# Three of four MLP up projections as seven half-size products in place of eight

## The reference

```python
hdn = rmsnorm(x, p["norm_mlp"][i]) @ p["w_up"][i]                 # 1024 -> 4096
x = x + (jnp.square(jax.nn.relu(hdn)) @ p["w_down"][i]).astype(x.dtype)   # 4096 -> 1024
```

## Time and profile before

| what | value |
|---|---|
| median of 3 runs | 2495.04 us (2494.24 to 2495.99) |
| the profiled execution, its own time | 2499.5 us |
| its span, first to last instruction | 2497.7 us |
| PE, DVE, ACT, POOL busy, share of the span | 98%, 39%, 42%, 18% |
| mean granted clock of PE | 0.996 of full speed |
| layer 0's MLP, in the chain of waits | 716.95 to 1252.04 us |
| POOL's accumulating DMAs of 256 KB, issue to landing | median 5.5 us, 504 issues |
| SP's raw chunk loads of 512 KB, issue to landing | median 3.9 us, 258 issues |

### The profile page before, as it was taken

One profiled execution on the slowest core, in us unless ns is written; L12 is line 12 of the kernel. 1 busy time (PEld: TensorE's weight loads), 2 busy tenths in 40 slices (PEclk: granted clock), 3 DMA queues, 4 the chain that ended last, 5 costly groups with the idle time before them and its releaser, 6 DMA issues.

```text
span 2497.7 us, 34597 instructions
## 1 busy us (share of the span) xinstructions
PE 2455.3 (98%) x13260; PEld 2061.6 (83%) x13260; DVE 973.5 (39%) x1372; ACT 1057.0 (42%) x1928; POOL 442.8 (18%) x512
## 2 busy tenths in 40 slices
PE   8999999999999999999999999999999999999996
PEld 6888578888888888888888885887878888888885
DVE  7877675104221111212378777630143211111124
ACT  5544536434443333434435435454344433333343
POOL 1111002220112122222111110023201222222210
PEclk9999999999999999999999999999999999999998
DMA  5544327863456666666555442378616566666664
GB/s 158 108 102 107 99 60 163 186 137 64 89 120 130 123 127 125 121 129 122 107 115 115 101 111 93 84 164 184 122 30 122 118 130 124 124 126 122 130 123 118
DMA packets 119789, 295.50 MB, mean 118 GB/s; under 512 B 13574, under 2 KB 13958, under 8 KB 119636
## 3 DMA queue, kind: packets, MB, share of 16 engines
q0 software_dynamic: 73152, 133.20, 31.9%
q1 hardware_dynamic: 46484, 160.20, 23.5%
HBM read 290.20 MB, written 3.15 MB: 117 GB/s over the span
## 4 chain that ended last, share of the span: by engine, by line
PE 94%; DVE 3%; DMA 2%; ACT 1%; issue 0%; SPq 0%; DVEq 0%; ACTq 0%
PE G L816 74%; PE M L1035 2%; PE G L1217 2%; PE M L775 2%; PE M L786 1%; PE M L788 1%; PE M L787 1%; PE G L1048 1%; PE M L1103 1%; DMA wlo<-wstream 1%; PE G L1013 1%; PE M L763 1%; PE M L932 1%; PE M L940 1%; PE M L831 0%
## 5 line engine op out<-in xcount | busy, mean ns | idle before, releaser
L425 ACT ACTIVATE wlo<-raw 128x512 fp32r<-128x512 f32 x508 | 320.6, 631 | 1101.7 <-PE G L816 1012.1
L411 POOL DMA_DIRECT2D wlo<-wstream x504 | 439.1, 871 | 1904.2 <-ACT wlo L425 1849.8
L816 PE MATMUL G<-A_lo,whi 128*128 128x256 f32 x1888 | 641.8, 340 | 0.0
L816 PE MATMUL G<-A_hi,whi 128*128 128x256 f32 x1888 | 605.8, 343 | 14.9 <-DVE A_lo L1326 9.1
L816 PE MATMUL G<-B_lo,whi 128*128 128x256 f32 (+1 forms) x1536 | 520.2, 339 | 0.0
L816 PE MATMUL G<-B_hi,whi 128*128 128x256 f32 (+1 forms) x1536 | 488.5, 340 | 0.0
L816 PE MATMUL G<-A_hi,wlo 128*128 128x256 f32 x1888 | 482.2, 337 | 0.0
L816 PEld LDWEIGHTS G<-A_hi,wlo 128*128 128x128 f32 x1888 | 356.3, 189 | 86.3
L816 PE MATMUL G<-B_hi,wlo 128*128 128x256 f32 (+1 forms) x1536 | 391.3, 336 | 0.0
L816 PEld LDWEIGHTS G<-A_lo,whi 128*128 128x128 f32 x1888 | 357.9, 190 | 38.7
L816 PEld LDWEIGHTS G<-A_hi,whi 128*128 128x128 f32 x1888 | 357.9, 190 | 21.4 <-issue 15.7
(11 more groups left out here) (304 smaller groups left out, 2436.3 us busy)
## 6 DMA issues: line engine op xcount, KB each, us to landing
raw<-wstream SPq DMA_DIRECT2D x258, 512.0 KB, 3.9
wlo<-wstream POOLq DMA_DIRECT2D x504, 256.0 KB, 5.5
ring<-dft SPq DMA_DIRECT2D x12, 512.0 KB, 3.8
mraw<-memT SPq DMA_DIRECT2D x16, 256.0 KB, 3.4
X<-xT SPq DMA_DIRECT2D x8, 384.0 KB, 6.9
win<-dft SPq DMA_DIRECT2D x6, 512.0 KB, 4.8
itab<-dft SPq DMA_DIRECT2D x6, 512.0 KB, 6.3
yT<-outs SPq DMA_DIRECT2D x8, 384.0 KB, 2.6
```

The source lines that it names most:

```text
L411: pool.dma_start(low, wstream[c][:, part], accum_op=ALU.add).then_inc(lo_in[c % 2][h], 16)
L425: act.activation(wlo[:, s, part], raw[:, s, part], ACT.Copy, scale=-1.0).then_inc(neg_done, 1)
L816: last = mm(out, w, p[:, k, a:b], start=(k == 0 and w is w_hi and p is parts[0]), stop=(k == KT - 1 and w is w_lo))
```

## The change

Quarter 0 of the MLP and all down tiles stay as they are. The up tiles of quarters 1, 2 and 3 of each layer go by groups: a group is two output tiles (256 hidden channels, two rows of `raw`), and takes the product of a 2x2 block weight (blocks of 128 outputs by 512 inputs) with a 2x2 block input (512 inputs by 384 tokens). The Strassen scheme (in Winograd's form) makes it of seven block products where eight are needed plainly. Each of the seven is 4 contraction blocks times three matmuls of 384 columns. A quarter is four groups, 28 products.

- **The inputs.** The norm's scale now goes onto the input: during the first four down tiles of quarter 0, DVE's `combine` makes the normalised input (`x_hat`) and four sums of its blocks (they become `T1` to `T4`) and, with ACT, the high and low parts of all seven input operands. They lie where `A_hi`, `A_lo` and the relu and hidden buffers were. They serve all three quarters.
- **The weights.** A product's weights lie in one of four half slots of `whi` and `wlo`, and are prepared when the product four places before has been used. Products 0, 4 and 6 of a group take a block as it is: negated copy on ACT, accumulating DMA on POOL (product 0's low part has a buffer of its own, `w_low`, prepared six products ahead). Products 1, 2, 3 and 5 take sums of blocks: DVE makes the sum in place in `raw`, ACT rounds it, DVE subtracts for the low part.
- **The results.** Products 0, 1, 2, 3 go to four PSUM banks, 4, 5, 6 are added onto banks 0, 2, 3. ACT copies products 0 and 1 out before 4 and 5 may write, DVE adds 2 and 3; then come the four hidden blocks of 128x384, each with a relu and square, a rounding copy on ACT and a subtraction on DVE.
- **The raw loads** come in pairs of rows, alternately in `raw` and a new `raw_b`.
- The loops over layers and quarters on SP, ACT and DVE are written out.

The core of the diff, with the indentation cut:

```diff
-CH = C_MLP + 16 * QUARTERS
+STREAM = C_MLP + 16 * QUARTERS
+FAST = QUARTERS - 1
+CH = STREAM - 8 * FAST
+LOADS = CH // 2 + 2 * FAST
 AHEAD = 2
 T_IN, T_OUT, T_K, T_Q, T_O, T_MLP = 0, 20, 28, 36, 44, 52
-TILES = T_MLP + 64
+TILES = T_MLP + 64 - 8 * FAST
...
+def combo(i):
+    o = oA + 12288 * i if i < 4 else oE + 12288 * (i - 4)
+    return tuple(place(f"mlp_{n}{i}", [P, 4, HALF_T], o + 6144 * j, F32R) for j, n in enumerate(("hi", "lo")))
+B11, B21, B22, T1, T2, T3, T4 = combos = [combo(i) for i in range(7)]
+x_hat = [place(f"x_hat{i}", [P, T], oE + 36864 + 3072 * i) for i in range(2)]
+t_one, t_two, t_three, t_four = acc[:, 0:HALF_T], acc[:, HALF_T:T], sq[:, 0:HALF_T], sq[:, HALF_T:T]
+raw_b = place("raw_b", [P, 2, D], oE + 36864)
+assert oE + 36864 + 8192 <= 229344
+p_one, p_five, v_sum = acc[:, 0:HALF_T], acc[:, HALF_T:T], sq[:, 0:HALF_T]
...
+def quad(p, row, col):
+    return pair_raw(p)[:, row, col * 512:(col + 1) * 512]
+def part_of(j):
+    return j % 4 // 2, slice(j % 2 * 512, j % 2 * 512 + 512)
...
-chunks(L, C_V0, CH - C_V0)
+chunks(L, C_V0, C_MLP + 16 - C_V0)
+for q in range(1, QUARTERS):
+    U, w = (L * FAST + q - 1) * 4, L * STREAM + C_MLP + 16 * q
+    def pair(p, buf, arrived):
+        for row in range(2):
+            if p > 1:
+                sp.wait_ge(u_dlo, 4 * (U + p - 2) + 4)
+                sp.wait_ge(u_hi, 7 * (U + p - 2) + (6, 7)[row])
+            sp.dma_start(buf[:, row, :], wstream[w + 2 * p + row]).then_inc(arrived[row], 16)
+    if q == 1:
+        sp.wait_ge(c_lo, 28 * (L + 1))
+    else:
+        sp.wait_ge(u_dlo, 4 * U)
+        sp.wait_ge(u_hi, 7 * U)
+    pair(1, raw_b, raw_b_in)
+    pair(2, raw, raw_in)
+    pair(3, raw_b, raw_b_in)
+    pair(4, raw, raw_in)
+    for m in range(8):
+        c = L * CH + C_MLP + 8 + 8 * q + m
+        sp.wait_ge(hi_done, c * 2 + 2)
+        sp.dma_start(raw[:, m % 2, :], wstream[w + 8 + m + AHEAD]).then_inc(raw_in[m % 2], 16)
...
+def first_low(p):
+    pool.wait_ge(u_neg1, U + p + 1)
+    pool.dma_start(w_low[:, :], wstream[w + 2 * p][:, 0:512], accum_op=ALU.add).then_inc(u_lo[0], 16)
+def later_low(p, i):
+    s, part = part_of(7 * p + (4, 6)[i])
+    pool.wait_ge(u_neg, 2 * (U + p) + i + 1)
+    pool.dma_start(wlo[:, s, part], wstream[w + 2 * p + i][:, 512:1024],
+                   accum_op=ALU.add).then_inc(u_lo[1 + i], 16)
+first_low(0)
+for p in range(4):
+    later_low(p, 0)
+    if p < 3:
+        first_low(p + 1)
+    later_low(p, 1)
+for m in range(8):
...
+for i, (src, ready) in enumerate(((x_hat[0][:, 0:HALF_T], 1), (x_hat[1][:, 0:HALF_T], 2), (x_hat[1][:, HALF_T:T], 2),
+                                  (t_one, 3), (t_two, 4), (t_three, 5), (t_four, 6))):
+    act.wait_ge(c_src, n + ready)
+    act.activation(combos[i][0][:, g, :], src, ACT.Copy).then_inc(c_hi, 1)
...
+def first_neg(q, p):
+    arrived, k = arrival(q, p)
+    act.wait_ge(arrived[0], 16 * (k + 1))
+    act.activation(w_low[:, :], quad(p, 0, 0), ACT.Copy, scale=-1.0).then_inc(u_neg1, 1)
+def weight_high(q, j):
+    U, (p, n) = (L * FAST + q - 1) * 4, divmod(j, 7)
+    s, part = part_of(j)
+    arrived, k = arrival(q, p)
+    U += p
+    if n == 6:
+        act.wait_ge(arrived[1], 16 * (k + 1))
+    if n in (1, 2, 3, 5):
+        act.wait_ge(u_s, 4 * U + (2, 1, 3, None, 4)[n - 1])
+    src = quad(p, *((0, 0), (1, 0), (0, 0), (0, 0), (0, 1), (0, 0), (1, 1))[n])
+    if n in (4, 6):
+        act.activation(wlo[:, s, part], src, ACT.Copy, scale=-1.0).then_inc(u_neg, 1)
+    act.activation(whi[:, s, part], src, ACT.Copy).then_inc(u_hi, 1)
+def fast_up(q):
+    U0 = (L * FAST + q - 1) * 4
+    for i in range(28):
+        U, n = U0 + i // 7, i % 7
+        bank = (GB, MB)[i // 7 % 2]
+        act.wait_ge(u_mm, 7 * U0 + i + 1)
+        if i < 24:
+            weight_high(q, i + 4)
+        else:
+            s, part = part_of(i)
+            if i % 2 == 0:
+                act.wait_ge(raw_in[s], 16 * (L * LOADS + (C_MLP + 16) // 2 + 6 * (q - 1) + 2 + 1))
+            act.activation(wlo[:, s, part], raw[:, s, part], ACT.Copy, scale=-1.0).then_inc(neg_done, 1)
+            act.activation(whi[:, s, part], raw[:, s, part], ACT.Copy).then_inc(hi_done, 1)
+        if n == 1 and i < 21:
+            first_neg(q, i // 7 + 1)
+        if n == 0:
+            act.wait_ge(u_c, 3 * U + 1)
+            act.activation(p_one, bank[0][:, 0:HALF_T], ACT.Copy).then_inc(u_p1, 1)
+        if n == 1:
+            act.activation(p_five, bank[2][:, 0:HALF_T], ACT.Copy).then_inc(u_p5, 1)
+        if n == 4:
+            act.activation(h_buf[1], bank[0][:, 0:HALF_T], ACT.Relu).then_inc(u_c11, 1)
+            act.wait_ge(u_c11, U + 1)
+            act.activation(h_buf[1], h_buf[1], ACT.Square).then_inc(u_sq, 1)
+            act.wait_ge(u_sq, U + 1)
+        if n >= 3:
+            k, half, buf, ready = ((1, 1, 0, 1), (0, 0, 1, None), (0, 1, 0, 2), (1, 0, 1, 3))[n - 3]
+            if ready is not None:
+                act.wait_ge(u_h, 3 * U + ready)
+            act.activation(B_hi[:, 2 * (i // 7) + k, half * HALF_T:(half + 1) * HALF_T], h_buf[buf],
+                           ACT.Copy).then_inc(u_hh, 1)
...
+    first = (C_MLP + 8) // 2 if q == 0 else (C_MLP + 16) // 2 + 6 * (q - 1) + 2
+    act.wait_ge(raw_in[s], 16 * (L * LOADS + first + (m + 2) // 2 + 1))
+    split(s, c + m)
+else:
+    if m == 6:
+        first_neg(q + 1, 0)
+    for h in range(2):
+        act.wait_ge((half_used, chunk_used)[h], c + m + 1)
+        weight_high(q + 1, 2 * s + h)
...
+def fast_up(q):
+    U0 = (L * FAST + q - 1) * 4
+    for p in range(4):
+        U, bank = U0 + p, (GB, MB)[p % 2]
+        for n, (src, b) in enumerate(((B11, 0), (T1, 2), (T3, 3), (T2, 1), (B21, 0), (B22, 2), (T4, 3))):
+            j = 7 * p + n
+            s, part = part_of(j)
+            if p == 0 and n == 0:
+                pe.wait_ge(psum_free, L * TILES + T_MLP + 16 + 8 * (q - 1) + 2)
+                pe.wait_ge(c_lo, 28 * (L + 1))
+            if p >= 2 and n < 4:
+                pe.wait_ge(*((u_c11, U - 1), (u_c, 3 * U - 3), (u_c, 3 * U - 2), (u_u1, U - 1))[n])
+            if n >= 4:
+                pe.wait_ge((u_p1, u_p5, u_v)[n - 4], U + 1)
+            pe.wait_ge(u_hi, 7 * U0 + j + 1)
+            if n in (0, 4, 6):
+                pe.wait_ge(u_lo[n // 3], 16 * (U + 1))
+            else:
+                pe.wait_ge(u_dlo, 4 * U + (1, 2, 3, None, 4)[n - 1])
+            out = bank[b][:, 0:HALF_T]
+            for k in range(4):
+                w = part.start + k * P
+                w_hi, w_lo = whi[:, s, w:w + P], wlo[:, s, w:w + P]
+                if n == 0:
+                    w_lo = w_low[:, k * P:(k + 1) * P]
+                mm(out, w_hi, src[0][:, k, :], start=(n < 4 and k == 0), stop=False, skip_group_check=n > 3)
+                mm(out, w_hi, src[1][:, k, :], start=False, stop=False, skip_group_check=n > 3)
+                last = mm(out, w_lo, src[0][:, k, :], start=False, stop=(k == 3), skip_group_check=n > 3)
+            last.then_inc(u_mm, 1)
+    pe.wait_ge(u_c11, U0 + 3)
+    pe.wait_ge(u_c, 3 * U0 + 10)
 up(L * CH + C_MLP, L * TILES + T_MLP, True)
-down(L * CH + C_MLP, L * TILES + T_MLP, L * 32)
+down(0)
 for q in range(1, QUARTERS):
...
+def combine(g):
+    n, k = (L * 4 + g) * 6, (L * 4 + g) * 7
+    if k:
+        dve.wait_ge(c_lo, k)
+    for i in range(2):
+        stt(out=x_hat[i][:, :], in0=X[:, g + 4 * i, :], scalar=par_("g_mlp", g + 4 * i), in1=rbc[:, :],
+            op0=ALU.mult, op1=ALU.mult).then_inc(c_src, 1)
+    b11, b12, b21, b22 = (x_hat[i][:, j * HALF_T:(j + 1) * HALF_T] for i in range(2) for j in range(2))
+    dve.wait_ge(c_src, n + 2)
+    tt(t_one, b12, b11, ALU.subtract).then_inc(c_src, 1)
+    dve.wait_ge(c_src, n + 3)
+    tt(t_two, b22, t_one, ALU.subtract).then_inc(c_src, 1)
+    tt(t_three, b22, b12, ALU.subtract).then_inc(c_src, 1)
+    dve.wait_ge(c_src, n + 4)
+    tt(t_four, b21, t_two, ALU.subtract).then_inc(c_src, 1)
+    for i, src in enumerate((b11, b21, b22, t_one, t_two, t_three, t_four)):
+        dve.wait_ge(c_hi, k + i + 1)
+        tt(combos[i][1][:, g, :], src, f(combos[i][0][:, g, :]), ALU.subtract).then_inc(c_lo, 1)
+def weight_low(q, j):
+    U, (p, n) = (L * FAST + q - 1) * 4, divmod(j, 7)
+    s, part = part_of(j)
+    a11, a12, a21, a22 = (quad(p, i, k) for i in range(2) for k in range(2))
+    if n == 1:
+        arrived, k = (raw_in, L * LOADS + (C_MLP + 16) // 2 + 6 * (q - 1) + p // 2) if p % 2 == 0 else \
+            (raw_b_in, (L * FAST + q - 1) * 2 + p // 2)
+        dve.wait_ge(u_neg1, U + p + 1)
+        dve.wait_ge(u_hi, 7 * (U + p) + 1)
+        dve.wait_ge(arrived[1], 16 * (k + 1))
+        tt(a11, a11, a21, ALU.subtract).then_inc(u_s, 1)
+        dve.wait_ge(u_s, 4 * (U + p) + 1)
+        tt(a21, a21, a22, ALU.add).then_inc(u_s, 1)
+    if n in (1, 2, 3, 5):
+        dve.wait_ge(u_hi, 7 * U + j + 1)
+        src = a21 if n == 1 else a11
+        tt(wlo[:, s, part], src, f(whi[:, s, part]), ALU.subtract).then_inc(u_dlo, 1)
+    if n == 2:
```

(112 more changed lines are left out.)

81 lines of the change are left out of this document (41 added, 40 removed).

## The result

The changed kernel takes 2512.46 us (median of 4 runs, 2509.48 to 2515.51) against 2494.64 us for the kernel before on the same chip: ratio 1.0072, 95% interval 1.0055 to 1.0089. It is slower by 18 us where 11 less were forecast, and outside the range (2507). The profiled execution took 2513.55 us, with a span of 2511.8.

A forecast was written before the change was run, and what follows sets the result against it. PE alone was taken to bound the MLP. A fast quarter: 1.3+59.0+5.0 = 65.3 us against 67.4, six times 12.6 less, 12 after 0.5 for odds and ends; 2495-12 = 2483, given as 2484, range 2466 to 2507.

The forecast's parts named there:

- PE's share of the sum: Matmuls in a fast quarter: 28 products of 2.11 us take 59.0 us against 67.4, 8.4 less.
- The ceiling: Most that PE's fewer matmuls could save over the six fast quarters: 50.6 us in all.
- Entry: Start of a fast quarter: product 0 waits for the last down tile's residual, 1.3 us, six times.
- Durations and the circuit: DVE and ACT operation times in a group; their fixed-order turns take 15.0 us against PE's 14.76, not deciding.
- Product 4: Its low part by DMA lands in 4.2 us; PE waits 1.0, 0.4 and 1.0 us in groups 1 to 3.
- Product 6: Its low part by DMA lands in 6.2 us; PE waits 1.1, 0.7 and 0.7 us in groups 0 to 2.
- Rival 4: PE's short idle times halve its clock; a fifth of six quarters at 1.2 GHz adds 71 us, 2555; chance 0.03.
- rival 1: Low parts reach PE too late before products 4 and 6, so it is slower: 2500 to 2510 us; chance 0.22.
- rival 2: Gain and loss cancel, with stalls of 6 to 8 us a quarter: 2495 us, within 5; chance 0.18.
- The `combine` of quarter 0: DVE's added work in quarter 0's down tiles, 8.6 us against a tile's 8.43; costed at nothing, possibly 2 us a layer.
- the delay weighed in the prediction: DVE operations with two SBUF inputs holding back POOL's issues: 0.35 us a group, 6 us in all; left out.
- SP's waits: Raw pair loads wait for rounding of products 5 and 6 two groups before; covered by some 8 us against 3.9.

The follow-up runs named there:

- e10: Changed kernel with low parts of products 0, 4 and 6 made on DVE, and product 0 waiting only for the seventh down tile's residual: 2444.81 us.
- e1: Changed kernel with SP's raw pair loads held until product 6's low part of two groups before has landed: 2478.47 us, ratio 0.9932 to the kernel before.
- e9: Changed kernel with only the second raw row of a pair held until product 6's low part of two groups before has landed: 2490.2 us.
- e2: Changed kernel with POOL issuing product 6's low part ahead of product 0's instead of after it: 2526.09 us, ratio 1.013 to the kernel before.

## Why the prediction was wrong

**PE's share of the sum was right.** Matmuls of 384 columns start 0.176 us apart (851.77, 851.95, 852.12), 28 products take 59 us. The ceiling, 2495-50.6 = 2444.4, is where e10 stands with the entry mended (2444.8).

**Entry: right.** 1.0 us of wait in each of six places, 8 to 9 us to be had by taking it away; 7.8 were costed.

**Durations and the circuit: right.** DVE at 384 columns takes 0.56 us, at 512 0.69. The circuit's turns came out within 0.3 us (e1). DVE and ACT are not what decides in the changed kernel: beside the entry no wait of PE is theirs. DVE was busy 42 us a quarter where 49 were expected, with 72 operations where the sum had 80, as a part of the weight work falls in the down tiles before.

**Product 4: its landing right (3.9 to 4.5 us against 4.2 taken), its wait out of place.** 2.4 us a quarter were costed for it, 14.4 in all. It stayed at nothing because product 6's delay of PE covered it; in e1, with that gone, it is 20.7 us, 1.5 to 2.1 in two places a quarter where 0.4 to 1.0 in three were worked out.

**Product 6: the step that failed.** "I take 6.2, a little above the 5.7 with one row beside" was the nearest row plus a half, for a transfer with two rows of 512 KB and another adding transfer around it. It was 7.2 to 8.4 us, median 7.4. In group 0 of the first fast quarter the issue came 7.6 us after the first matmul (7.5 worked out), the landing was 8.40 and the wait 3.2 instead of 1.1. In the groups after it the prediction had the negated copy behind the circuit; as PE had been held, it followed product 2 directly instead, and the wait is then the same each time: from product 2's end 0.2 to ACT, 0.64 copy, 0.28 to the issue, 7.4 landing, 0.13 to PE, less three products of 2.11, is 2.3. The sum of these waits is 41.6 us against 15.0 costed for product 6 and 29.4 for both. e1 shows the cause by taking away the loads beside it (34 us gained, landings back to 5.3 at most), e9 prices one row, e2 excludes the place in POOL's list. The Trainium skill ("DMA: Bandwidth & Descriptors", issuing engines are not separate DMA queues) says that loads started by SP and by POOL run on the same DMA engines; these landings agree.

**The clock: the second step that failed, a term put at nothing.** Rival 4 was given 0.03 because the earlier trace rows had 1.00 granted with PE busy 12.9 of 17 us. Most of what PE stood still there is a single wait of 3.1 us, and ten of the 18 waits here left the clock alone too, so one such row couldn't exclude the fall. Here it fell behind eight waits of 2.0 to 2.5 us, for some 3.4 us at a time: 13 us in the rows above, not 71. The Trainium skill's rule on the clock ("TensorE: Matmul & The Clock Gate", the HAM clock gate), that an idle PE is set back to half its clock, speaks against this change, and the trace agrees in eight of 18 waits and not in the other ten.

**The account.** A fast quarter is 1.3 + 59.1 + 41.6/6 + 13.4/6 = 69.6 us. The residuals that end one quarter and the next, less eight down tiles of 8.43, say 69.7 on average (the six distances 139.46, 134.84, 137.88, 137.75, 136.23 and 136.42 us). The forecast had 65.3. 4.4 more, six times, is 26 of the 28 us between 2484 and 2512. Of these 26, 11.6 are waits (41.6 against the 30 costed) and 13.4 the clock, so the clock is the larger half of the miss. The waits are 6.9 us a quarter, just under the 7.1 from which rival 1 decides: alone they are rival 2, gain and loss cancel. The prediction's own walk through a quarter, with product 6's landing at 7.4 and its copy straight behind product 2, gives 2.3 us three times, the same 6.9. What makes it slower, and takes it past the range's end, is 13 us of rival 4's mechanism on top. So rival 1 named the outcome and the place (its 0.7 us more on each landing was 1.3 on product 6's on average, none on product 4's), but not the whole path; the chances were 0.22, 0.18 and 0.03.

**Costed at nothing, rightly.** The `combine` of quarter 0, DVE's operations beside POOL's issues (865 ns, minimum and median, with DVE busy 42 of 70 us: the delay weighed in the prediction didn't show), SP's waits: PE waits for none of them.

## What to carry to other kernels

When a change shortens the lead of a transfer, price its landing with everything that the same change starts in the same few microseconds, not by the median of a stream in which it ran nearly alone; and if the loads beside it have slack, hold them back, for one wait on SP here was worth 34 us. A small wait that recurs in the middle of dense matmuls may cost the clock as well, so it counts for more than its own length. Where VectorE stands half idle, a low part made on it from operands already in SBUF (0.69 us) beats a copy, an issue and a landing (5 to 9 us).
